# A two-layer transformer kernel on one core: the last layer norm spread over ScalarE, GpSimd and VectorE, and the output stored in half tiles

## What is computed

```
for l in range(DEPTH_2):                       # 2 layers
    mix = token_mixers(x, ...)
    x = layer_norm(DN_ALPHA * x + mix, ln1_g[l], ln1_b[l])
    ffn = grouped_moe(x, ...)
    x = layer_norm(DN_ALPHA * x + ffn, ln2_g[l], ln2_b[l])
return x                                       # (1, 256, 1024)
```

## Time and profile before

| | |
|---|---|
| three runs | 2204.47 to 2211.40 us, median 2207.65 us |
| the profiled execution's own time | 2207.64 us |
| its span in the trace | 2205.8 us |
| TensorE busy | 2076.7 us, 94% |
| VectorE busy | 1159.4 us, 53% |
| ScalarE busy | 767.2 us, 35% |
| GpSimd busy | 63.5 us, 3% |
| granted TensorE clock, mean | 0.978 |

### The profile page before, as it was taken

One profiled execution on the slowest core, in us unless ns is written; L12 is line 12 of the kernel. 1 busy time (PEld: TensorE's weight loads), 2 busy tenths in 40 slices (PEclk: granted clock), 3 DMA queues, 4 the chain that ended last, 5 costly groups with the idle time before them and its releaser, 6 DMA issues.

```text
span 2205.8 us, 28498 instructions
## 1 busy us (share of the span) xinstructions
PE 2076.7 (94%) x11724; PEld 1636.6 (74%) x11724; DVE 1159.4 (53%) x1729; ACT 767.2 (35%) x1183; POOL 63.5 (3%) x98
## 2 busy tenths in 40 slices
PE   5999999999999999999999799999899999899996
PEld 3677787888897699889998655556599987555563
DVE  4333333377784265565656633357666466423475
ACT  3111122355433144444443222234335432212251
POOL 0000000010010000000001100000000002000000
PEclk8999999999999999999999999999999999899998
DMA  9655523122341345434423179989453332689894
GB/s 367 257 218 218 205 77 124 38 77 77 119 169 77 147 166 180 165 139 155 153 98 132 52 290 376 379 336 384 184 180 134 115 134 71 241 338 379 336 387 187
DMA packets 55328, 433.60 MB, mean 197 GB/s; under 512 B 7328, under 2 KB 8608, under 8 KB 17696
## 3 DMA queue, kind: packets, MB, share of 16 engines
q1 hardware_dynamic: 51344, 423.35, 50.2%
q10 hardware_dynamic: 3856, 8.42, 1.1%
HBM read 430.71 MB, written 1.05 MB: 196 GB/s over the span
## 4 chain that ended last, share of the span: by engine, by line
PE 56%; issue 35%; DVE 5%; DMA 2%; ACT 1%; DVEq 1%; POOL 0%; POOLq 0%; SPq 0%; ACTq 0%
PE bank L2894 33%; PE bank L3639 4%; PE bank L2887 3%; PE bank L3637 3%; PE bank L3690 2%; PE bank L2830 1%; PE bank L3701 1%; PE bank L3050 1%; DMA ring<-in_l_moe_in 1%; PE bank L3688 1%; PE bank L3563 1%; DMA ring<-in_early 1%; PE bank L3654 1%; DVE ring_lo L2748 1%; DVE X L2738 1%
## 5 line engine op out<-in xcount | busy, mean ns | idle before, releaser
L2894 PE MATMUL bank<-HT_LO,ring_lo 128*128 128x256 f32 (+1 forms) x992 | 287.6, 290 | 0.0
L2894 PE MATMUL bank<-X_HI,ring_lo 128*128 128x256 f32 x1472 | 270.7, 284 | 2.1 <-issue 2.1
L2894 PE MATMUL bank<-HT_HI,W_HI 128*128 128x512 f32 (+1 forms) x704 | 238.7, 339 | 7.0 <-DVE ring_lo L1915 4.0
L2894 PE MATMUL bank<-HT_HI,ring_lo 128*128 128x512 f32 (+1 forms) x704 | 240.3, 341 | 0.0
L2894 PE MATMUL bank<-HT_LO,W_HI 128*128 128x512 f32 (+1 forms) x704 | 238.3, 339 | 0.0
L2894 PEld LDWEIGHTS bank<-X_HI,ring_lo 128*128 128x128 f32 x1472 | 230.6, 190 | 3.9 <-issue 3.8
L1199 ACT ACTIVATE W_HI<-ring 128x2048 fp32r<-128x2048 f32 x66 | 126.3, 1914 | 285.2 <-PE bank L2894 225.7
L2894 PEld LDWEIGHTS bank<-HT_LO,ring_lo 128*128 128x128 f32 x992 | 187.9, 189 | 3.2 <-issue 0.5
L1915 DVE TENSOR_TENSOR ring_lo<-ring,W_HI 128x2048 fp32r<-128x2048 f32 x66 | 151.0, 2288 | 66.0 <-ACT W_HI L1199 65.9
L2282 DVE TENSOR_TENSOR ring_lo<-ring,ring_lo 128x2048 fp32r<-128x2048 f32 (+2 forms) x64 | 143.2, 2247 | 42.3 <-ACT ring_lo L1452 41.2
L2894 PEld LDWEIGHTS bank<-HT_HI,W_HI 128*128 128x128 f32 x704 | 133.5, 190 | 28.6 <-issue 9.8
(11 more groups left out here) (541 smaller groups left out, 3708.7 us busy)
## 6 DMA issues: line engine op xcount, KB each, us to landing
ring<-in_early SPq DMA_DIRECT2D x54, 2048.0 KB, 8.4
ring<-in_l_moe_in SPq DMA_DIRECT2D x36, 2048.0 KB, 14.1
ring<-in_l_dense SPq DMA_DIRECT2D x62, 1024.0 KB, 4.9
ring<-in_l_moe_out SPq DMA_DIRECT2D x14, 2048.0 KB, 13.9
ring<-in_early SPq DMA_DIRECT2D x23, 1024.0 KB, 4.7
slot<-in_l_moe_in SPq DMA_DIRECT2D x10, 2048.0 KB, 10.1
slot_xg<-in_l_moe_in SPq DMA_DIRECT2D x10, 2048.0 KB, 12.0
HT<-in_l_moe_in SPq DMA_DIRECT2D x8, 2048.0 KB, 9.1
```

Of the source, the lines that this page charges most:

```text
L2894: last = mm(out, a, b, start=start and n == 0, stop=stop and n == 2)
```

## The change

The last norm of the last layer is no longer done by VectorE alone.

- VectorE no longer normalises tile 0 between the adds of (1,0) and (1,1) in the last layer.
- GpSimd computes `-mean` of tile 0, its rstd, and their product `ln_bias` (`last_half`), and raises `last_scaled`.
- ScalarE normalises all of tile 0 in one pass, scale `ln_rstd`, bias `ln_bias` (L1693 of the changed kernel), and raises `last_normed`.
- GpSimd multiplies the first half of tile 0 by the gain row, computes the rstd of tile 1, and adds the bias row; ScalarE's queue stores that half.
- VectorE does tile 1 in fused passes over halves: `(X - mean) * G2` on two halves without waiting for rstd, then, behind the second half of tile 0 (one multiply, one add), `X * rstd + G3` on two halves.
- SP stores the other three halves, 256 KB each.
- A tile `ln_bias` of two columns is allocated behind `ln_rstd`, and four semaphores are added. Every tile named after it starts 32 bytes later: `HT` at 128608 instead of 128576, `slot4` at 199264 instead of 199232, in bytes of a partition.

```
@@ memory and semaphores
         ln_rstd = sb("ln_rstd", [P, 2])
+        ln_bias = sb("ln_bias", [P, 2])
...
+        last_scaled = sem("last_scaled")
+        last_normed = sem("last_normed")
+        last_out = sem("last_out")
+        last_out_pool = sem("last_out_pool")
@@ SP
-            for t in range(2):
-                sp.wait_ge(ln_done, 4 * LAYERS - 1 + t)
-                sp.dma_start(io["out"][t * P:(t + 1) * P, :], X[:, t, :]).then_inc(out_stored, 16)
-            sp.wait_ge(out_stored, 16 * 2)
+            for i, (t, half) in enumerate(((0, 1), (1, 0), (1, 1))):
+                cut = slice(half * BANK, half * BANK + BANK)
+                sp.wait_ge(last_out, i + 1)
+                sp.dma_start(io["out"][t * P:(t + 1) * P, cut], X[:, t, cut]).then_inc(out_stored, 16)
+            sp.wait_ge(out_stored, 16 * 4)
@@ ScalarE, last layer
+                    se.wait_ge(last_scaled, 1)
+                    act(X[:, 0, :], X[:, 0, :], ACT.Identity, scale=ln_rstd[:, 0:1], bias=ln_bias[:, 1:2]).then_inc(last_normed, 1)
+                    se.wait_ge(last_out_pool, 1)
+                    se.dma_start(io["out"][0:P, 0:BANK], X[:, 0, 0:BANK]).then_inc(out_stored, 16)
@@ GpSimd, last layer instead of ln_scale(1)
+                    po.wait_ge(variance_ready, L * 4 + 3)
+                    po.tensor_scalar(ln_bias[:, 0:1], ln_mean[:, 0, 0:1], -1.0, None, ALU.mult)
+                    po.tensor_tensor(ln_rstd[:, 0:1], ln_rstd[:, 0:1], neghalf[:, 0:1], ALU.pow)
+                    po.drain()
+                    po.tensor_tensor(ln_bias[:, 1:2], ln_bias[:, 0:1], ln_rstd[:, 0:1], ALU.mult).then_inc(last_scaled, 1)
+                    half = X[:, 0, 0:BANK]
+                    po.wait_ge(rows2_loaded, L * 32 + 32)
+                    po.wait_ge(last_normed, 1)
+                    po.tensor_tensor(half, half, G[:, 2, 0:BANK], ALU.mult)
+                    po.wait_ge(variance_ready, L * 4 + 4)
+                    po.tensor_tensor(ln_rstd[:, 1:2], ln_rstd[:, 1:2], neghalf[:, 0:1], ALU.pow).then_inc(ln_rstd_ready, 1)
+                    po.drain()
+                    po.tensor_tensor(half, half, G[:, 3, 0:BANK], ALU.add).then_inc(last_out_pool, 1)
@@ VectorE
-                    if (t, half) == (1, 0):
+                    if (t, half) == (1, 0) and L < LAYERS - 1:
                         normalise_tokens(0, 1)
...
+                    first, second = slice(0, BANK), slice(BANK, D)
+                    ve.wait_ge(rows2_loaded, L * 32 + 32)
+                    for cut in (first, second):
+                        stt(X[:, 1, cut], X[:, 1, cut], ln_mean[:, 1, 0:1], G[:, 2, cut], ALU.subtract, ALU.mult)
+                    ve.wait_ge(last_normed, 1)
+                    tt(X[:, 0, second], X[:, 0, second], G[:, 2, second], ALU.mult)
                     ve.drain()
-                    residual(L, [0])
-                    normalise_tokens(1, 1)
-                    ve.drain()
-                    residual(L, [1])
+                    tt(X[:, 0, second], X[:, 0, second], G[:, 3, second], ALU.add).then_inc(last_out, 1)
+                    ve.wait_ge(ln_rstd_ready, L * 4 + 3)
+                    for cut in (first, second):
+                        stt(X[:, 1, cut], X[:, 1, cut], ln_rstd[:, 1:2], G[:, 3, cut], ALU.mult, ALU.add).then_inc(last_out, 1)
```

More of the change, by code:

```diff
@@ L1684, in _ @@
                     normed_features(J_XT3)
+                else:
+                    se.wait_ge(last_scaled, 1)
+                    act(X[:, 0, :], X[:, 0, :], ACT.Identity, scale=ln_rstd[:, 0:1], bias=ln_bias[:, 1:2]).then_inc(last_normed, 1)
+                    se.wait_ge(last_out_pool, 1)
+                    se.dma_start(io["out"][0:P, 0:BANK], X[:, 0, 0:BANK]).then_inc(out_stored, 16)
         @block.gpsimd
@@ L1770, in ln_scale, with last_half @@
                         po.tensor_tensor(ln_rstd[:, t:t + 1], ln_rstd[:, t:t + 1], neghalf[:, 0:1], ALU.pow).then_inc(ln_rstd_ready, 1)
+                def last_half():
+                    po.wait_ge(variance_ready, L * 4 + 3)
[11 more added lines that the diff above has]
+                    po.tensor_tensor(half, half, G[:, 3, 0:BANK], ALU.add).then_inc(last_out_pool, 1)
                 ln_scale(0)
-                ln_scale(1)
+                if L < LAYERS - 1:
+                    ln_scale(1)
+                else:
+                    last_half()
         @block.vector
```

## The result

| | before | changed |
|---|---|---|
| median of ten runs | 2207.57 us | 2212.58 us |
| lowest to highest | 2204.47 to 2211.57 us | 2210.63 to 2214.90 us |
| ratio, 95% interval | | 1.0021, 1.0012 to 1.0030 |
| span of the profiled execution | 2205.8 us | 2210.8 us |
| start of the variance of tile 0 (L2556, now L2586) | 2192.66 | 2199.30 |

The last two lines of times split the result. All that the diff changes in the instruction streams lies behind the variance of tile 0, and there the changed kernel is 1.64 us faster. But it comes to that point 6.64 us later, though no instruction ahead of it was changed. These are two single executions; the medians give the same split, 5.0 us lost in all and so 6.6 lost ahead of the tail, with an interval of some 4.3 to 8.3.

What follows compares the result with a forecast made beforehand. TensorE was taken as busy 94% of the span, with the change confined to the last 14 us, bound mainly by VectorE. 0.90 us at VectorE's end plus 0.45 for the store gave 1.35, so 2206.3 us, range 2202.5 to 2209.0.

Steps and rivals of the forecast that it cites:

- The pass that leaves VectorE: Tail: without tile 0's normalising pass on VectorE, the add of (1,1) and all behind it come 0.71 us earlier.
- ScalarE's and GpSimd's chain: Tail: GpSimd's scale and bias out at 2194.10, ScalarE's pass 1.08 us, GpSimd's half able to start at 2195.35.
- VectorE's six passes with turns: Tail: six passes of 512 columns alternate with GpSimd's; VectorE ends 0.90 us earlier, 2.71 without collisions.
- The rival without collisions: Tail: VectorE and GpSimd overlap fully, six passes in 3.9 us, 2204.2 us in all; chance 0.15.
- the one in which GpSimd comes last: Tail: VectorE always takes the interface, GpSimd's add ends behind VectorE's last pass; 2206.2 us, or 2207.5; chance 0.12.
- The store: End of tail: last piece 256 KB instead of 512, gain between 0 and 0.73 us, taken as 0.45.
- The formula of the Trainium skill: Last store: some 2.0 us plus bytes over 436 GB/s, by which halving the piece would save 0.60 us.
- the bounds of 0.3 to 3.44: Tail gain in us: from later hand-overs and no store gain up to full overlap and full store gain.
- Other edits: the semaphores and the few instructions cost nothing.: Ends of instruction streams: semaphores and few instructions cost nothing, as no engine has anything behind them.
- Slower: the shifted tiles: Expert stage: loads to `HT` and `slot4`, shifted 32 bytes, become dearer by 7.6% or more; 2214.3 us; chance 0.05.
- The numbers: Whole kernel: 2206.3 us, range 2202.5 to 2209.0; chance 0.89 of staying within 0.3% of no change.
- The tensor_scalar rule: Tail: the variance's last instruction, L2586, might be held behind GpSimd's multiply, slipping all by 0.2 us to 2206.5.

Runs made afterwards that it cites:

- e1: The changed kernel with `ln_bias` allocated behind every other tile, so that no address moves; 2207.41 us, ratio 1.0004 to the kernel before.
- e6: The changed kernel, later tiles 64 bytes further than before, last norm in fused VectorE passes, without ScalarE's pass and GpSimd's half; 2202.91 us, ratio 0.9976 to the kernel before.
- e9: The kernel before with 32 unused bytes ahead of `W_HI` (`HID_HI` moves along); one execution, 2209.59 us beside 2210.87.
- e10: The kernel before with 64 unused bytes ahead of `W_HI` (`HID_HI` moves along); one execution, 2209.67 us beside 2210.87.
- e5: The changed kernel, later tiles 64 bytes further than before, GpSimd's half given to VectorE; one execution, 11.20 us from the variance of tile 0 to the end.

## Why the prediction was wrong, by its steps

- **The pass that leaves VectorE.** 0.71 us forecast, 0.73 measured. Its six passes then began 0.08 us before the recorded end of the variance, where the sum had them 0.09 behind it: another 0.17 gained.
- **ScalarE's and GpSimd's chain.** ScalarE's pass took 1.24 us, not 1.08; GpSimd's product of one column 0.19, not 0.27. GpSimd's multiply started 2.74 us behind the start of the variance, forecast 2.69.
- **VectorE's six passes with turns.** Forecast 5.71 us, measured 5.48, and 3.9 without collisions. VectorE's second pass was forecast behind GpSimd's power and ran beside it. One turn went the other way, at 2204.4: the forecast had GpSimd's add, which waited first, go first; VectorE's multiply ran free and its add was held instead. So the sum came near by errors of both signs, in part by luck. The rival without collisions is refuted, and so is the one in which GpSimd comes last: its store was issued at 2206.26, ahead of VectorE's last two passes (2206.71).
- **The store.** 0.45 forecast, 0.32 measured. The formula of the Trainium skill that the prediction quotes stands in a section on transfers issued by GpSimd, and these are SP's; stores of half the size landed 2.2 us after their issue instead of 2.6, so 0.4 less and not 0.60. Together the tail: 1.35 forecast, 1.64 measured (1.32 up to VectorE's end, 0.90 forecast), within the bounds of 0.3 to 3.44.
- **"Other edits: the semaphores and the few instructions cost nothing." This is the step that failed.** It is true of those: e1, which has them all, shows no loss (1.0004, 0.9992 to 1.0017). But the sum left out the one edit that decided, the 32 bytes of `ln_bias`, a term of some 6.6 us against the tail's 1.35; it stood among the rivals only, with a chance of 0.05.
- **"Slower: the shifted tiles".** The place was right and the mechanism wrong. I priced it on loads to `HT` and the slots, which didn't change (9.0 and 9.9 us), and asked for 7.6% on them. The price was on TensorE's pace, 1% on the group of three (693 to 700 ns) and 0.5% over all matched products, in a program in which TensorE is busy 94% of the span. That row was in front of me: 1% of such a program is 20 us, and a tenth of that undoes the tail's gain.
- **The numbers.** 2206.3 us and 2202.5 to 2209.0 were built on the tail alone; the time came out 3.6 us above the range. That the difference stays within 0.3% was right, 0.21%, but because a loss of 6.6 was set against a gain of 1.6, which no case of mine had.
- **The tensor_scalar rule.** The Trainium skill, page "SBUF — State Buffer", section "Who interferes with whom", lets a tensor_scalar collide as well, on conditions for its operands. L2586 ran at 2202.56 beside GpSimd's multiply (2202.04 to 2203.30) in 0.15 us, as ever: for one column it did not apply here.

## What to carry to other kernels

A new tile, however small, is a change to every tile allocated behind it. Put it last, or measure the layout by itself with an unused tile in the old kernel; where TensorE bounds a kernel, a scan of such shifts within 256 bytes is a cheap experiment, worth 0.5% here between the worst and the best. And before sharing elementwise work between VectorE and GpSimd, count the VectorE passes with two on-chip inputs: each waits its turn with GpSimd's passes. Fusing alone (e6) took 1.5 us off VectorE's end, the change with its moved passes 1.3.

## What the runs showed of the hardware that was not expected

- In this program the pace of TensorE depends on where its operands start, as far as seen modulo 256 bytes: 22.02, 22.42 or 22.62 us for the same 96 products of 512 columns. Shifts that differ by 256 bytes (0 and 256, 64 and 320) gave the same median paces within 1 ns, except where few products count.
- With all starts alike (128 modulo 256, the ring's), 512 columns are fastest (227 ns) and 256 columns slowest (120 ns against 117 to 119). Whether another common start does the same, and whether a layout can have both, was not tried.
- A product's pace changes when only an operand of its neighbours moves (e9, e10, and `X_HI,ring_lo` in every shift). Why is open.
- GpSimd waits for a VectorE pass with two on-chip inputs even with an instruction of one column: its power took 0.55 us alone, 1.00 behind a VectorE pass of 512 columns and 1.52 behind one of 1024. It isn't waited for: VectorE's next pass took 0.74 us beside it, as long as a free one, in the changed kernel, e5 and e6.
